# Expert gates in two 256-column products a pair of tokens, their one-hot rows from GpSimd

## The reference, cut to what matters

```
top_s, pos = lax.top_k(cand_s, PEER_TOPK)
eidx = jnp.take_along_axis(cand_i, pos, axis=-1)
gate = jax.nn.softmax(top_s, axis=-1).astype(xb.dtype)
h = jax.nn.gelu(jnp.einsum('thkd,td->thk', u[eidx], xb), approximate=False)
return jnp.einsum('thk,thkd->td', gate * h, v[eidx])
```

## Time and profile before

| | before |
|---|---|
| median of 3 runs | 2551.2 us (2549.73 to 2558.75) |
| the profiled execution's span | 2553.6 us |
| the profiled execution's own time | not shown apart from its span |
| stretch with gates, first expert layer | about 434 to 697 us |
| stretch with gates, second expert layer | about 1390 to 1654 us |

### The profile page before, as it was taken

The page is one execution under the profiler, slowest core; times in us unless marked ns, Lnnn a source line. Parts: engine busy times, 40 slices in busy tenths (PEclk is TensorE's granted clock), DMA queues, the critical chain, the costliest instruction groups (busy, mean ns, idle before and its releaser), DMA issues.

```text
span 2553.6 us, 41919 instructions
## 1 busy us (share of the span) xinstructions
PE 2458.0 (96%) x16535; PEld 2233.5 (87%) x16535; DVE 1790.3 (70%) x3178; ACT 1207.0 (47%) x1803; POOL 265.6 (10%) x124
## 2 busy tenths in 40 slices
PE   7998999999999999988999999999999899999999
PEld 7867999999988888777999999988888788787997
DVE  5576696888766677756696888766767667555675
ACT  4344445444555554444445455455454564435433
POOL 0000485000000000000485000000000102000000
PEclk9999999999999999989999999999999999899999
DMA  7544587666677777542587666677777542143655
GB/s 233 172 128 149 186 228 221 192 187 188 197 244 265 241 235 244 167 127 97 181 230 223 188 188 191 193 247 255 245 239 244 185 132 91 62 138 124 182 163 176
DMA packets 201426, 483.66 MB, mean 189 GB/s; under 512 B 24080, under 2 KB 93712, under 8 KB 200720
## 3 DMA queue, kind: packets, MB, share of 16 engines
q1 hardware_dynamic: 197920, 473.46, 59.7%
q10 hardware_dynamic: 3312, 7.53, 0.9%
HBM read 446.30 MB, written 34.60 MB: 188 GB/s over the span
## 4 chain that ended last, share of the span: by engine, by line
PE 87%; DVE 8%; ACT 2%; issue 1%; DMA 1%; ACTq 0%; SPq 0%; DVEq 0%
PE psum L1019 29%; PE psum L1065 26%; PE psum L817 22%; PE psum L1042 4%; DVE rounded L1524 2%; PE psum L1183 2%; ACT rounded L2576 1%; DMA sb<-in_ret_w_in 1%; PE psum L1000 1%; PE psum L949 1%; DVE sb L1559 0%; DVE sb L1580 0%; PE psum L1149 0%; PE psum L1151 0%; PE psum L1442 0%
## 5 line engine op out<-in xcount | busy, mean ns | idle before, releaser
L1524 DVE TENSOR_TENSOR rounded<-sb,rounded 128x1024 fp32r<-128x1024 f32 (+3 forms) x696 | 813.9, 1172 | 548.8 <-ACT rounded L2959 322.4
L2959 ACT ACTIVATE rounded<-sb 128x1024 fp32r<-128x1024 f32 x512 | 543.0, 1061 | 758.6 <-PE psum L1019 361.8
L1019 PE MATMUL psum<-rounded 128*128 128x256 f32 x6144 | 767.4, 284 | 0.0
L1019 PEld LDWEIGHTS psum<-rounded 128*128 128x128 f32 x6144 | 743.6, 191 | 0.0
L1065 PE MATMUL psum<-rounded,weights 128*128 128x512 f32 x3072 | 698.1, 389 | 2.0 <-DVE weights L2506 1.7
L1065 PEld LDWEIGHTS psum<-rounded,weights 128*128 128x128 f32 x3072 | 576.2, 188 | 123.3 <-issue 2.9
L817 PE MATMUL psum<-rounded 128*128 128x256 f32 (+1 forms) x3924 | 590.0, 312 | 32.5 <-DVE rounded L1524 20.9
L817 PEld LDWEIGHTS psum<-rounded 128*128 128x128 f32 x3924 | 540.5, 194 | 78.3 <-DVE rounded L1524 22.3
L2576 ACT ACTIVATE rounded<-sb 128x1024 fp32r<-128x1024 f32 (+4 forms) x280 | 265.7, 954 | 396.1 <-PE psum L817 283.6
L790 POOL TENSOR_TENSOR rounded<-sb,rounded 128x1024 fp32r<-128x1024 f32 x96 | 237.5, 2479 | 484.5 <-ACT rounded L2959 484.0
L2497 DVE TENSOR_TENSOR halves<-halves,small 128x768 bf16<-128x768 bf16 x256 | 131.5, 555 | 4.4
(11 more groups left out here) (388 smaller groups left out, 1475.3 us busy)
## 6 DMA issues: line engine op xcount, KB each, us to landing
sb<-in_u_turned SPq DMA_DIRECT2D x256, 512.0 KB, 3.9
sb<-in_peer_v SPq DMA_DIRECT2D x256, 512.0 KB, 3.5
hidden<-sb SPq DMA_DIRECT2D x256, 128.0 KB, 3.9
sb<-hidden SPq DMA_DIRECT2D x256, 128.0 KB, 3.3
sb<-in_ret_w_in SPq DMA_DIRECT2D x48, 512.0 KB, 3.9
sb<-in_ffn_w_up SPq DMA_DIRECT2D x40, 512.0 KB, 4.0
sb<-in_peer_w_q SPq DMA_DIRECT2D x32, 512.0 KB, 3.8
sb<-in_ffn_w_down SPq DMA_DIRECT2D x22, 512.0 KB, 4.2
```

Of the source, the lines that this page charges most:

```text
L1019: mm = pe.matmul(ps(bank, 1)[:, 0:T], u[p][:, k * P:(k + 1) * P], hT[:, q, k, :], start=(k == 0 and w == 0), stop=(k == KD - 1 and w == 2))
L1524: vec.tensor_tensor(ring_lo[0:k, part, 0:wide], ring[0:k, slot, 0:wide], ring_hi[0:k, part, 0:wide].bitcast(F32), ALU.subtract).then_inc(c ...
L2959: act.activation(ring_hi[:, n % SPLIT, :], ring[:, n % RING, :], ACT.Copy).then_inc(tile_hi, 1)
```

## The change

Only the making of the gate table in the two expert layers.

- The tokens go in pairs: 128 groups of two a layer, group g behind tile 47 + 3g/5 (two, two and one group behind three tiles).
- The gate is split into two parts, a rounded 32-bit one and the rest, instead of three bf16 parts; all one-hot rows are 32-bit (fp32r).
- The one-hot rows of i and j are made by GpSimd (`pool_pairs`): four instructions of 128 elements a pair, each comparing the row 0 to 127 with a token's column of i or j. It begins after its 48 lowerings and when `take_routes` has marked `routes_known`. There are three buffers; it waits for `onehots_used` from the fourth pair on and marks `pairs_made`.
- VectorE's `onehots` is one instruction a pair: the one-hot rows of i times the two gate parts of both tokens (128x512). It waits for `pairs_made` and stands ahead of the lowering in VectorE's order.
- TensorE makes one product of 256 columns a token: j's one-hot rows as weights, both gate parts side by side as columns. So the two parts are no longer summed in PSUM. The products go in turn to banks 4, 5, 0, 1.
- ScalarE's `place` copies the first half into G (128x256) and marks `gates_begun`; VectorE's new `place` adds the second half from PSUM to it (128x256), behind the lowering of the tile, and marks `gates_placed`.

```diff
-GROUPS = T // 4
+GROUPS = T // 2
...
+GATE_BANKS = (4, 5, 0, 1)
...
-        halves = nc.alloc_sbuf_tensor_at("halves", [P, 5120], BF16, offset=SB_AT + 4 * pair_at)
-        half_parts = Memory(halves, 0, 5120)
-        ij_onehot = half_parts.take(2, 2, 4, P)
-        gate_onehot = half_parts.take(2, 3, 2, P, 2)
+        pairs = nc.alloc_sbuf_tensor_at("pairs", [P, 2560], F32R, offset=SB_AT + 4 * pair_at)
+        pair_parts = Memory(pairs, 0, 2560)
+        ij_onehot = pair_parts.take(3, 2, 2, P)
+        gate_onehot = pair_parts.take(2, 2, 2, P)
...
-            group_after.setdefault(FIRST_GROUP + g * 6 // 5, []).append(g)
+            group_after.setdefault(FIRST_GROUP + g * 3 // 5, []).append(g)
...
+            def pool_pairs(phase):
+                base = gates_before[phase]
+                gp.wait_ge(routes_known, peers_before[phase] + 1)
+                for g in range(GROUPS):
+                    if g >= 3:
+                        gp.wait_ge(onehots_used, base + g - 2)
+                    for q in range(2):
+                        for w in range(2):
+                            last = gp.tensor_scalar(ij_onehot[:, g % 3, w, q], iota, routes_ij[:, w, 2 * g + q:2 * g + q + 1], None, ALU.is_equal)
+                    last.then_inc(pairs_made, 1)
...
                 def gates(g):
-                    buf = g % 2
+                    bank = GATE_BANKS[g % 4]
                     pe.wait_ge(onehots_made, base + g + 1)
-                    if g < 2:
-                        hold([4 + buf])
+                    if g < 4:
+                        hold([bank])
                     else:
-                        pe.wait_ge(gates_placed, base + g - 1)
-                    for q in range(4):
-                        for p in range(3):
-                            mm = pe.matmul(ps(4 + buf, 1)[:, q * P:(q + 1) * P], ij_onehot[:, buf, 1, q, :],
-                                           gate_onehot[:, buf, p, q // 2, :, q % 2], start=(q == 0 and p == 0), stop=(p == 2),
-                                           skip_group_check=True)
+                        pe.wait_ge(gates_placed, base + g - 3)
+                    for q in range(2):
+                        mm = pe.matmul(ps(bank, 1)[:, q * T:(q + 1) * T], ij_onehot[:, g % 3, 1, q, :],
+                                       gate_onehot[:, g % 2, q].rearrange("p a b -> p (a b)"), start=(q == 0), stop=True,
+                                       skip_group_check=True)
                     mm.then_inc(onehots_used, 1)
...
-                vec.tensor_copy(iota_half, iota).then_inc(*own.next())
-                vec.tensor_copy(iota_two, bcast(iota, 2, 2)).then_inc(*own.next())
...
                 def onehots(g):
...
                     if g >= 2:
                         vec.wait_ge(onehots_used, base + g - 1)
...
+                    vec.wait_ge(pairs_made, base + g + 1)
+                    vec.tensor_tensor(gate_onehot[:, g % 2].rearrange("p q w c -> p w q c"), bcast(ij_onehot[:, g % 3, 0].bitcast(F32), 1, 2),
+                                      bcast(routes_g[:, :, 2 * g:2 * g + 2].bitcast(F32), 3, P), ALU.mult).then_inc(*own.mark(onehots_made))
+
+                def place(g):
+                    vec.wait_ge(gates_begun, base + g + 1)
+                    two = ps(GATE_BANKS[g % 4], 1).rearrange("p (q w i) -> p w i q", q=2, w=2)
+                    vec.tensor_tensor(G[:, :, 2 * g:2 * g + 2], two[:, 1], G[:, :, 2 * g:2 * g + 2], ALU.add).then_inc(*own.mark(gates_placed))
...
                 for i in range(BY_POOL - 3, 2 * NK):
+                    for g in group_after.get(i + 1, []):
+                        onehots(g)
                     if i + 3 < 2 * NK:
                         lower_tile(first_u + i + 3)
+                    for g in group_after.get(i, []):
+                        place(g)
...
-                    for g in group_after.get(i + 2, []):
-                        onehots(g)
...
                 def place(g):
                     act.wait_ge(onehots_used, base + g + 1)
-                    act.activation(G[:, :, 4 * g:4 * g + 4], ps(4 + g % 2, 1).rearrange("p (q i) -> p i q", q=4),
-                                   ACT.Copy).then_inc(gates_placed, 1)
+                    two = ps(GATE_BANKS[g % 4], 1).rearrange("p (q w i) -> p w i q", q=2, w=2)
+                    act.activation(G[:, :, 2 * g:2 * g + 2], two[:, 0], ACT.Copy).then_inc(gates_begun, 1)
```

More of the change, by code:

```diff
@@ L350, in build @@
         ring_lo = split_parts.take(SPLIT, SLOT)
-        halves = nc.alloc_sbuf_tensor_at("halves", [P, 5120], BF16, offset=SB_AT + 4 * pair_at)
-        half_parts = Memory(halves, 0, 5120)
-        ij_onehot = half_parts.take(2, 2, 4, P)
-        gate_onehot = half_parts.take(2, 3, 2, P, 2)
+        pairs = nc.alloc_sbuf_tensor_at("pairs", [P, 2560], F32R, offset=SB_AT + 4 * pair_at)
+        pair_parts = Memory(pairs, 0, 2560)
+        ij_onehot = pair_parts.take(3, 2, 2, P)
+        gate_onehot = pair_parts.take(2, 2, 2, P)
         hid = Memory(sb, pair_at + 2560, 768).take(3, T)
         full = Memory(sb, pair_at + 2560, 512).take(2, T)
[L359 to L364, removed]
+        routes_ij = Memory(nc.alloc_sbuf_tensor_at("routes_ij", [P, 2 * T], BF16, offset=SB_AT + 4 * (pair_at + 3328)), 0, 2 * T).take(2, T)
+        routes_g = Memory(nc.alloc_sbuf_tensor_at("routes_g", [P, 2 * T], F32R, offset=SB_AT + 4 * (pair_at + 3584)), 0, 2 * T).take(2, T)
         hid_back = Memory(sb, pair_at, 1024).take(4, T)
@@ L396, in build @@
         onehots_made, onehots_used = sem("onehots_made"), sem("onehots_used")
+        routes_known, pairs_made, gates_begun = sem("routes_known"), sem("pairs_made"), sem("gates_begun")
         gates_placed = sem("gates_placed")
@@ L791, in _ @@
                                          ALU.subtract).then_inc(pool_split, 1)
+                    pool_pairs(phase)
                 if phase == "mixers":
@@ L2468, in take_routes @@
                 def take_routes():
-                    rest = a["rest"]
                     vec.wait_ge(psum_for_vec, psum_v.up())
-                    for w in range(2):
-                        vec.tensor_copy(routes[:, w, :], ps(0, 1)[:, w * T:(w + 1) * T]).then_inc(*own.next())
+                    vec.tensor_copy(routes_ij.rearrange("p w t -> p (w t)"), ps(0, 1)).then_inc(*own.mark(routes_known))
                     g = ps(1, 1)[:, 0:T]
-                    vec.tensor_copy(routes[:, 2, :], g).then_inc(*own.next())
+                    round_to(routes_g[:, 0], g).then_inc(*own.next())
@@ L2475, in take_routes @@
                     done()
[L2476 to L2482, removed]
+                    vec.tensor_tensor(routes_g[:, 1], g, routes_g[:, 0].bitcast(F32), ALU.subtract).then_inc(*own.mark(vec_served))
@@ L2483, in take_routes @@
                     done()
                 def onehots(g):
-                    buf, t = g % 2, slice(4 * g, 4 * g + 4)
                     if g >= 2:
                         vec.wait_ge(onehots_used, base + g - 1)
-                    i_pairs = ij_onehot[:, buf, 0].rearrange("p a b -> p (a b)").rearrange("p (q c two) -> p q c two", q=2, two=2)
-                    of_pair = routes[:, 0, t].rearrange("p (q two) -> p q two", two=2)
-                    vec.tensor_tensor(i_pairs, bcast(iota_two, 1, 2), bcast(of_pair, 2, P), ALU.is_equal).then_inc(*own.next())
```

## The result

The change makes the kernel slower: 2819.84 us as the median of 4 runs (2818.11 to 2822.58) against 2551.17 (2549.73 to 2558.75), a ratio of 1.1046 with a 95% interval of 1.1029 to 1.1063. The prediction had the direction (2586) and not the size; the range, up to 2651, misses by far.

A forecast was written before the change was run, and what follows sets the result against it. TensorE was taken to bound the kernel before, GpSimd and VectorE excluding each other on SBUF after: 287.4 us a layer, 17.6 more than today, 35 in all; 2553.6 + 35.0 less 2.4 gives 2586 us, range 2514 to 2651.

The forecast's parts named there:

- The price d: Duration of one GpSimd comparison of 128 elements in the expert layers, taken as 0.35 us.
- The high end: Upper estimate for one GpSimd comparison, from subtractions of two operands: 2.2 ns an element and 0.13 fixed, so 0.41 us.
- The nearest row, the copy: GpSimd's copy of 128 elements, one operand like the comparison, read as 0.28 us alone.
- Rival (c): GpSimd's comparison costs above 0.41 us because of the scalar's fetch; at 0.45, 2689 us; chance 0.12.
- The sum for the lock: GpSimd and VectorE instructions that exclude each other on SBUF operands, less overlaps: 108.2 + 512 d, 287.4 us a layer.
- The mechanism: In the gate stretches VectorE waits for GpSimd's pairs, its lowering comes late, TensorE waits for its tile; 17.6 us a layer.
- TensorE's saving: TensorE's 77 tiles with gates fall from 269.8 to 252.5 us a layer if it stays the bound; 34.6 in all.
- Rival (d): TensorE's wide gate product of 256 columns does not run at 0.120 us; chance 0.01.
- Edits at nothing: Small edits around the first gates, such as dropped index copies and fewer casts: -2 to +4 us over both layers, 0 taken.

The follow-up runs named there:

- product from PSUM: Changed kernel with the gate parts kept in a PSUM bank, so VectorE's 128x512 product reads one operand there, and three gate banks instead of four; 2722.1 us.
- copies: Changed kernel with each GpSimd comparison replaced by a plain copy of the row 0 to 127, same count and size; 2525.7 us.
- constant scalar: Changed kernel with GpSimd comparing against the constant 3.0 instead of a token's column, same number and size of instructions; 2687.8 us.
- comparisons of 256: Changed kernel with two GpSimd comparisons of 256 elements a pair instead of four of 128, both tokens against the first one's index; 2645.0 us.
- the version that beats both: Changed kernel with GpSimd lowering tiles up to 125, VectorE making one-hot rows in wide instructions with one PSUM operand, two hidden banks; 2519.8 us in 6 runs.

## Why the prediction was right in direction and wrong in size

**The price d failed.** "I take 0.35, halfway from the copy to the high end", with 0.21 and 0.41 as the ends. It is 0.597. The high end was no bound: I took it from two-operand instructions, 2.2 ns an element and 0.13 fixed, in the belief that one operand and a scalar could not cost more than two operands. The comparison costs 2.5 ns an element and 0.275 fixed. (The 1.265 in that fit is also a multiplication, L773, not a subtraction, and the longest of four of its shape; the others took 1.046 to 1.088.) The nearest row, the copy, was read nearly right (0.28 against 0.293) and is another kind of instruction at half the price. Rival (c), a dearer comparison, is what happened, beyond its 0.45 and for another reason than it gave: the fetch of the scalar is 0.074 of 0.597.
At 0.597, 0.578 from start to start, GpSimd alone needs 296 us a layer, more than today's 269.8, so by the estimate above the change loses 52 us before any collision.

**The sum for the lock was about right for this kernel, in part by luck, and not in general.** 108.2 + 512 x 0.597 = 413.9 us a layer gives 2551.2 + 2 x (413.9 - 269.8) = 2839, against 2820 measured. So with the right price the step that turns it into time would have been 19 us off. The same sum by the measured prices of four experiments:

| kernel | sum a layer, us | time by it | measured |
|---|---|---|---|
| product from PSUM (only the lowering excluded) | 94.3 - 77 x 0.27 + 512 x 0.597 - 435 x 0.06 = 353.1 | 2718 | 2722 |
| copies | 108.2 + 512 x 0.293 = 258.2 | 2528 | 2526 |
| constant scalar | 108.2 + 512 x 0.523 = 376.0 | 2764 | 2688 |
| comparisons of 256 | 182.0 - 55.4 + 256 x 0.919 - 51 x 0.06 = 358.8 | 2729 | 2645 |

It comes near for two and is 76 and 84 us too high for the others; the copies are a weak test of it, because TensorE is the bound there (busy 255.76 of 256 us, GpSimd 252.88). What GpSimd loses beyond its undisturbed time, (0.803 - 0.597) x 512 = 105 us a layer in the changed kernel, is 58% of VectorE's 182; with the constant scalar 81 us, 45%. The sum charges 127, 70%. It took each product and each lowering as a wait of its own, less 0.27. In the traces a comparison that is under way runs on to its end beside VectorE, and only the next one waits, so a product alone costs GpSimd 0.20 of its 0.78; the loss is as large as it is here because 76 comparisons a layer wait for a product and a lowering in one. Against that, the sum took 0.06 for the overlap of two comparisons, which is 0.02. The two errors go opposite ways. The Trainium skill's "SBUF — State Buffer", section "Who interferes with whom", says that a VectorE instruction with two SBUF inputs contends with a GpSimd instruction that reads SBUF. The traces agree that such operands collide and that one PSUM operand ends it (0.783 to 0.688 for the product), while the total was never the whole 182.

**The mechanism held, one link apart.** "VectorE waits for pairs, the lowering behind that wait comes late, and TensorE waits for its tile": VectorE does wait, 342.6 us in all, but TensorE is caught earlier, at the gate product of the pair itself (192.8 us for L2488). That product stands ahead of the next tile in TensorE's order, so the lowering's three tiles of lead never come into it.

**TensorE's saving was right.** A tile and the two pairs behind it take 505.85 - 502.49 = 3.36 us in the version that beats both: 2.88 + 4 x 0.120, as taken. Rival (d) falls. Of the 34.6 us promised, that version shows 2550.3 - 2519.8 = 30.5.

**Edits at nothing.** ScalarE's copy took 0.399, not 0.365, and VectorE's addition 0.430, not 0.418; both stay hidden in all runs where TensorE is the bound. The 268.7 us measured less the 264 of the comparisons leaves 5 for the start and the end of the stages, 1 above the -2 to +4 allowed, which is less than the spread of the kernel before (9 us).

The range failed with d: it reached to the high end and left out "(c)" as unlikely, because "nothing in the rows speaks for it". Nothing spoke against it either: no row showed that kind of instruction on that engine.

## What to carry to other kernels

Price an instruction by a row of its own kind on its own engine; where there is none, a row of another kind is an example and no bound, and with 512 of them in a layer each 0.1 us is 51 us. Give an engine with a large fixed price few large instructions, and the many small ones to none if they can be made in one wide instruction. Where GpSimd and VectorE both work out of SBUF, their own times do not tell whether they fit side by side (with half of the comparisons on each, GpSimd's went from 0.595 to 1.110), and it counts how VectorE's instructions follow each other: a product and a lowering in one go held a comparison up by 1.25, apart by 0.94. One operand in PSUM took the product out of that.

## What the runs showed of the hardware

- On GpSimd a comparison with a scalar takes 0.597 us for 128 elements and 0.919 for 256; a constant scalar saves 0.074; subtracting costs what comparing costs (0.602, its mean 0.807 against 0.803); a copy takes 0.293. The Trainium skill's "GPSIMD Engine Reference", section "Engine selection", calls work with one input roughly line rate there. One element a cycle at that page's 1.2 GHz is an estimate of 0.83 ns; the measured 2.5 ns is three times that, and the measurement decides.
- The granted clock of the stretch fell to 0.91 in the changed kernel and to 0.90 with the product from PSUM, between the 1.2 and the 2.4 GHz level on the mean, where TensorE had idled between short bursts; it stayed at 1.00 with constant scalars, although TensorE idled there too (253 busy of 320 us). The rows of the last two, product from PSUM first:

```profile
440.00:780.00 340.00, 276.61 (x2016) 270.84 (x2015) 217.32 (x323) 136.76 (x271) 339.52 (x494) 0.90 0.49 144
440.00:760.00 320.00, 253.13 (x2006) 242.99 (x2005) 218.86 (x318) 138.53 (x269) 320.00 (x490) 1.00 0.52 152
```

  In all three GpSimd is busy for the whole stretch or all but 0.5 us of it, so the clock costs little here; what made it fall in two and not in the third, no run shows.
